# Per-row norm factor moved from the inputs to the exits of two projections, and the memory norm moved among the gate products

## The reference, cut to what matters

```python
# end of the first block
ple_gate = jax.nn.sigmoid(rms_norm(x, g_ple) @ w_ple_gate)
x = x + ple_gate * (p @ w_ple_proj)

# second block
mem_n = rms_norm_2(mem, mem_norm)
hn = rms_norm_2(h, norm_pre[0])                     # h = x
k_m, v_m = split(mem_n @ w_mem_kv[i])               # for both layers i
c_q, c_kv, k_r, q_m, gate = split(hn @ w_in_a)      # 384, 256, 32, 256, 1024 columns
main = mla_mixer(c_q, c_kv, k_r, ...)
mem_out = softmax(q_m @ k_m.T / 8) @ v_m            # 4 heads, 256 memory tokens
...
```

## Time and profile before

| | us |
|---|---|
| median of 3 runs (lowest, highest) | 3482.05 (3481.04, 3482.25) |
| the profiled execution | 3481.96 |
| its span | 3480.2 |
| TensorE busy | 3105.8 (89%) |
| VectorE busy | 1777.9 (51%) |
| ScalarE busy | 1185.4 (34%) |
| GpSimd busy | 1085.8 (31%) |
| mean granted TensorE clock | 0.953 |

### The profile page before, as it was taken

One profiled execution on the slowest core, in us unless ns is written; L12 is line 12 of the kernel. 1 busy time (PEld: TensorE's weight loads), 2 busy tenths in 40 slices (PEclk: granted clock), 3 DMA queues, 4 the chain that ended last, 5 costly groups with the idle time before them and its releaser, 6 DMA issues.

```text
span 3480.2 us, 36734 instructions
## 1 busy us (share of the span) xinstructions
PE 3105.8 (89%) x14488; PEld 2561.2 (74%) x14488; DVE 1777.9 (51%) x1804; ACT 1185.4 (34%) x1880; POOL 1085.8 (31%) x426
## 2 busy tenths in 40 slices
PE   5888799999999999999886898899976689999997
PEld 4666578887878888888676677688855567777786
DVE  5888943112253444444675334577744746656533
ACT  2666720001131000000322223577742425555511
POOL 2111034444424444444245232111122022121152
PEclk9999999999999999999898998999997899999998
DMA  2000021112101111111112111200031110000131
GB/s 94 19 25 31 19 91 49 49 49 93 46 31 49 49 49 49 49 49 49 43 49 106 34 67 52 79 31 25 31 127 43 49 37 26 30 25 31 55 115 67
DMA packets 44572, 178.99 MB, mean 51 GB/s; under 512 B 4672, under 2 KB 5696, under 8 KB 43392
## 3 DMA queue, kind: packets, MB, share of 16 engines
q1 hardware_dynamic: 32976, 119.89, 10.9%
q10 hardware_dynamic: 11440, 56.89, 4.2%
HBM read 147.40 MB, written 29.36 MB: 51 GB/s over the span
## 4 chain that ended last, share of the span: by engine, by line
PE 72%; DVE 11%; issue 10%; ACT 5%; POOL 2%; DMA 1%; SPq 0%; ACTq 0%; DVEq 0%; POOLq 0%
PE ps L456 47%; PE ps L1022 4%; PE aux L933 3%; PE ps L872 2%; PE ps L917 2%; PE ps L576 2%; PE ps L478 1%; PE ob L500 1%; PE ob L952 1%; PE ob L955 1%; PE ob L953 1%; PE aux L935 1%; DVE eb L1811 1%; POOL wh L413 1%; PE aux L605 1%
## 5 line engine op out<-in xcount | busy, mean ns | idle before, releaser
L413 POOL TENSOR_TENSOR wh<-raw,con 128x1024 fp32r<-128x1024 f32 x211 | 510.3, 2419 | 2334.1 <-PE ps L456 1198.9
L415 POOL TENSOR_TENSOR wl<-raw,wh 128x1024 fp32r<-128x1024 f32 x211 | 575.3, 2727 | 16.6
L456 PE MATMUL ps<-hh,wh 128*128 128x512 f32 x1536 | 479.7, 394 | 29.0 <-POOL wl L415 11.3
L456 PE MATMUL ps<-hl,wh 128*128 128x512 f32 x1536 | 477.4, 392 | 0.0
L456 PE MATMUL ps<-hh,wl 128*128 128x512 f32 x1536 | 476.4, 391 | 0.0
L456 PEld LDWEIGHTS ps<-hh,wh 128*128 128x128 f32 x1536 | 289.9, 190 | 92.1 <-issue 18.4
L456 PEld LDWEIGHTS ps<-hl,wh 128*128 128x128 f32 x1536 | 291.3, 190 | 61.4
L456 PEld LDWEIGHTS ps<-hh,wl 128*128 128x128 f32 x1536 | 291.0, 189 | 61.3
L1669 DVE TENSOR_TENSOR px_l<-px,px_h 128x512 fp32r<-128x512 f32 (+3 forms) x288 | 214.0, 745 | 115.4 <-ACT px_h L1526 113.3
L1909 DVE TENSOR_TENSOR y_t<-y_t,ps 128x1024 f32<-128x1024 f32 x120 | 146.5, 1220 | 174.6 <-PE ps L456 174.6
L1259 ACT ACTIVATE ff<-fr 128x1024 f32<-128x1024 f32 x32 | 34.0, 1061 | 552.9 <-DVE fr L1898 552.9
(11 more groups left out here) (353 smaller groups left out, 6291.3 us busy)
## 6 DMA issues: line engine op xcount, KB each, us to landing
raw<-wall SPq DMA_DIRECT2D x211, 512.0 KB, 3.5
spill_x<-x_t ACTq DMA_DIRECT2D x2, 4096.0 KB, 12.7
spill_out<-ot ACTq DMA_DIRECT2D x16, 512.0 KB, 2.6
go<-spill_out ACTq DMA_DIRECT2D x16, 512.0 KB, 5.8
xold_t<-spill_x ACTq DMA_DIRECT2D x2, 4096.0 KB, 16.4
x_t<-xt SPq DMA_DIRECT2D x8, 512.0 KB, 8.5
spill_o<-op ACTq DMA_DIRECT2D x4, 1024.0 KB, 3.9
o_all<-spill_o ACTq DMA_DIRECT2D x2, 2048.0 KB, 12.6
```

Source lines behind the costliest of these rows:

```text
L413: pool.tensor_tensor(wh[:, s, :, :], raw[:, s, :, :], ones.unsqueeze(1).broadcast_to([P, KT, P]), ALU.mult).then_inc(w_high, 1)
L415: pool.tensor_tensor(wl[:, s, :, :], raw[:, s, :, :], wh[:, s, :, :].bitcast(F32), ALU.subtract).then_inc(w_split, 1)
L456: m = pe.matmul(ps[:, w, a:b], lw[:, sl, k, :], r[:, i, a:b], start=(i == 0 and j == 0), stop=(i == len(ks) - 1 and j == 2))
```

## The change

- The gate products and the second block's first projection read x*g instead of x*g*r: `hh` is made on ACT straight from x and g (`Identity` with a scale), `hl` on DVE (`ple_low`, `scalar_tensor_tensor` of x, g and `hh`). The row is copied once to SBUF (`ple_row`, `a_row`) and multiplied in where a product leaves PSUM, now on DVE (`ple_scaled`, `q_scaled`, `scaled_out`, `gate_scaled`).
- The tiles `hh`, `hl` are made within `update`, so the gate products start tile by tile; the sums of the last two squares go between the k tiles (`with_late_sums`), the row between the last tile's two halves.
- The projection of `p` is taken out earlier, to `pp` (eight buffers of their own).
- The memory norm is done after the fourth gate product's exit (m = 3 on DVE and ACT, before the sixth k tile of gate product 4 on TensorE), with its own small buffers `mnt`.
- `hh`, `hl` for the second block are made while gate product 7 still reads the old ones (semaphore `gate_tile`, per k tile). Its two query products come before the memory products, and one by one.
- The memory values are computed with `m_h` as the stationary operand and the weights moving, 48 matmuls of 128 columns (`memory_values`), and need no transpose. The pads of the queries are cleared within that stretch.
- `cq`, `ckv`, the rope key and the gates of layer 0 leave by DVE.

```diff
@@ TensorE
-        norm_stats(KT, S, slab_next=True)
-        nready = norm_tiles(KT)
-        two_products(hh, hl, nready)
-        for _ in range(KT - 2):
-            product(range(KT), hh, hl)
-        pe.wait_ge(macc_ready, 1)
-        clear_sums(0)
-        column_sums(m_acc, N_MEM, 0).then_inc(mstat_done, 1)
-        tile_sums(KT, S, 1)
...
+        two_products(hh, hl, with_late_sums(norm_tiles(KT)), between=lambda: norm_row(S))
+        for m in range(2, KT):
+            product(range(KT), hh, hl, ready=(lambda i: norm_row(N_MEM) if i == 5 else None) if m == 4 else None,
+                    read=gate_tile if m == KT - 1 else None)
+            if m == 2:
+                pe.wait_ge(macc_ready, 1)
+                clear_sums(1)
+                column_sums(m_acc, N_MEM, 1).then_inc(mstat_done, 1)
+
+        mready, ready = norm_tiles(KT), norm_tiles(KT)
+        product(range(KT), hh, hl, ready=with_late_sums(ready))
+        product(range(KT), hh, hl, ready=lambda i: norm_row(S) if i == 1 else None)
         for layer in range(2):
             for j in range(2):
-                product(range(KT), m_h, m_l, n=N_MEM, ready=ready)
...
+                product(range(KT), m_h, m_l, n=N_MEM, ready=mready)
+                mready = None
             for j in range(2):
-                w = product(range(KT), m_h, m_l, n=N_MEM)
-                evacuated(w)
-                transposes(mv, 2, slab_next=(layer == j == 1))
+                memory_values()
@@ VectorE
+        def ple_low(k, gain=V_PLE):
+            dve.wait_ge(nh_ready, t.next(nh_ready))
+            dve.scalar_tensor_tensor(out=hl[:, k, :], in0=x_t[:, k, :], scalar=vcol(gain + k),
+                                     in1=hh[:, k, :].bitcast(F32), op0=ALU.mult, op1=ALU.subtract).then_inc(norm_ready, 1)
...
+        for i in range(2):
+            zero_pads(pads[i])
+            q_scaled(i)
+        for i in range(8):
+            memory_out(i)
...
+        def scaled_out(dst):
+            w, slot = work()
+            dve.tensor_tensor(dst, ps[:, slot, :], a_row[:, :], ALU.mult).then_inc(work_free[slot], 1)
...
-        skip()
+        gate_scaled(5, gt_late)
         w, slot = work()
+        chain(dve.tensor_tensor(ps[HI, slot, :], ps[HI, slot, :], a_row[HI, :], ALU.mult))
         norm(cq_t, 3, S, V_QN, cq_h, cq_l)
```

More of the change, by code:

```diff
@@ L460, in proj, with product, memory_values, two_products @@
                             t.fresh = False
+                if read is not None and k != ks[-1]:
+                    m.then_inc(read, 1)
             m.then_inc(work_done, 1)
-        def product(ks, rh, rl, n=S, ready=None, sl=None):
+        def product(ks, rh, rl, n=S, ready=None, sl=None, read=None):
             sl = slab() if sl is None else sl
             w, slot = work()
-            proj(slot, sl, ks, rh, rl, n, ready)
+            proj(slot, sl, ks, rh, rl, n, ready, read)
             return w
-        def two_products(rh, rl, ready, begun=True):
+        def memory_values():
+            sl = slab()
+            w, slot = work()
+            for kb in range(2):
+                rows = slice(kb * P, (kb + 1) * P)
+                for k in range(KT):
+                    for j, (l, r) in enumerate(((m_h, wh), (m_l, wh), (m_h, wl))):
+                        m = pe.matmul(ps[:, slot, rows], l[:, k, rows], r[:, sl, k, :],
+                                      start=(k == 0 and j == 0), stop=(k == KT - 1 and j == 2))
+                        if t.fresh:
+                            m.then_inc(slab_begun, 1)
+                            t.fresh = False
+            m.then_inc(work_done, 1)
+        def two_products(rh, rl, ready, begun=True, between=None):
             slabs, slots = [slab(), slab()], [work()[1], work()[1]]
@@ L483, in two_products @@
                         m.then_inc(work_done, 1)
+                        if between and i == 0:
+                            between()
         def transposes(src, n, slab_next=False):
@@ L1679, in norm_row, with square_adder @@
             dve.wait_ge(row_done, t.next(row_done))
-        def square_adder(ktiles):
+        def square_adder(ktiles, late=1):
             first = t.take("sq", ktiles)
+            total = acc if ktiles == KT else cq_acc
             def add(k):
@@ new lines, in _, with ple_scaled, ple_added @@
+        update(y_t, x_t, x_t, V_POSTMLP, low_part=ple_low, squares=square_adder(KT, 2))
+        ple_low(KT - 1)
+        skip(KT)
+        norm_row(S)
+        chain(dve.tensor_copy(ple_row[:, :], row[:, :]))
+        def ple_scaled(m):
+            w, slot = work()
+            if m >= 2:
+                dve.wait_ge(tile_ready, tiles + m - 1)
+            dve.tensor_tensor(pg[m % 2][:, :], ps[:, slot, :], ple_row[:, :], ALU.mult).then_inc(work_free[slot], 1)
+        def ple_added(m):
+            dve.wait_ge(ple_ready, m + 1)
+            chain(dve.tensor_tensor(pg[m % 2][:, :], pg[m % 2][:, :], pp[m], ALU.mult))
+            dve.tensor_tensor(x_t[:, m, :], x_t[:, m, :], pg[m % 2][:, :], ALU.add).then_inc(tile_ready, 1)
@@ L1932, in _ @@
             if m > 1:
                 squares(m - 1)
-        barrier(dve, t, dve_end)
-        norm(m_t, KT, N_MEM, V_MEM, m_h, m_l)
+            if m == 3:
+                norm_row(N_MEM, 1)
+                norm_tiles(m_t, KT, N_MEM, V_MEM, m_h, m_l, tmp=mnt)
+                t.take(norm_ready, KT)
+            if m == KT - 2:
+                for k in range(KT - 2):
+                    ple_low(k, V_PRE2)
+        ple_low(KT - 1, V_PRE2)
+        norm_row(S)
+        chain(dve.tensor_copy(a_row[:, :], row[:, :]))
@@ new lines, in q_scaled @@
+        def q_scaled(n):
+            w, slot = work()
+            for h, rows in ((0, LO), (1, HI)):
+                i = dve.scalar_tensor_tensor(out=q_f[n][rows, h, :], in0=ps[rows, slot, :], scalar=SCALE_64,
+                                             in1=a_row[rows, :], op0=ALU.mult, op1=ALU.mult)
+            i.then_inc(work_free[slot], 1)
+            dve.wait_ge(high_ready, t.next(high_ready))
+            for h, rows in ((0, LO), (1, HI)):
+                low(pads[n][1][rows, h, :], q_f[n][rows, h, :], pads[n][0][rows, h, :])
```

208 lines of the change are left out of this document (127 added, 81 removed).

## The result

| | before | after |
|---|---|---|
| median (lowest, highest), 15 runs each, us | 3482.12 (3478.40, 3488.31) | 3490.63 (3485.83, 3498.34) |
| the profiled execution, its span, us | 3481.96, 3480.2 | 3489.53, 3487.6 |
| mean granted TensorE clock | 0.953 | 0.948 |

The ratio is 1.0025, 95% interval 1.0018 to 1.0032: 8.5 us slower, just above what I called no change and 0.6 us above my range. I had forecast 4 us faster.

A forecast was written before the change was run, and what follows sets the result against it. TensorE, busy 89% of the span, was taken as the bound, so only its waits and low clock could be won. Terms -14.4 up to the scores, +1.3 and +9.0 gave -4.1: 3478.0 us, range 3465 to 3490.

The forecast's parts named there:

- the price of a value matmul: Memory values: 0.11 to 0.13 us for each of 48 matmuls, so 6.1 us a product (first 7.0).
- The marks of my sum: Predicted start times on TensorE, moved one after another; the memory scores at 1932.4 against 1946.86.
- The rival that I wrote down with this mechanism: Value products run at the low clock, 0.22 us a matmul, 17 us more: 3495; chance 0.15.
- the last mark: Start of the first latent product, after the memory attention; predicted shift -4.1 us.
- Up to the third gate product: Stretch ending where the third gate product starts: 9.5 us earlier, at 1764.8 against 1774.31.
- The memory norm: Norm within gate product 4: 5.9 us lost, with 3.8 of wait and 1.0 for a lower clock.
- The chain of the exits: Queries: DVE's row copy, pad clears, scaling and remainders free slot 1 at P+60, when the second key product starts.
- The attention: Memory attention: 1.3 us lost; five gate spills each 0.27 later behind DVE's exits, 1.35.
- My 1.5 back for a warm start: Memory attention: starting with TensorE warm returns the 1.5 us of loading the exponential's table at the first maximum.
- After it: After the memory attention: 9.0 us lost, from gate 5's exit behind the angles, rope key scaling and later gate exits.
- the clock rival: Value products at the low clock, 0.22 us a matmul, 17 us more: 3495; chance 0.15.
- The prediction's title for the stretch after the gate products: Heading for the stretch from the gate products' end to the memory attention: 10.5 us won.

The follow-up runs named there:

- e5_before_direct: Kernel before with only its memory value products replaced by 48 matmuls of 128 columns, no copy or transposes: 3496.55 us, ratio 1.0043.
- e6_before_wide: Kernel before with only its memory value products replaced by direct ones of 256 moving columns: 3486.06 us, ratio 1.0009.
- e1_turned: Kernel after with memory values again computed as 24 matmuls of 256 columns, copied out by ScalarE and transposed: 3471.84 us, ratio 0.9971.
- e2_wide: Kernel after with the 48 value matmuls taking 256 moving columns in place of 128, for all but the last input block: 3475.34 us, ratio 0.9980.

## Why the prediction was wrong

- **The failed step** is the price of a value matmul: "I take 0.11 to 0.13, as each matmul has its own load and keys, half idle, ran mostly at the high clock." Measured: 0.21 for nearly all of them. My own upper bound, "the low clock on a weight-bound stream, 3.55/16 = 0.22", from column sums in that very stretch, was the right row. I chose the row of the attention, where such matmuls are few and stand among wide ones, and leaned on keys that are 256 columns wide. The marks of my sum held 25.4 us for the four, the first at 7.0; the two pairs took 19.7 and 19.9. With these in their place the scores come 0.2 us earlier than before; the trace has 0.9 later. The rival that I wrote down with this mechanism, its price (17 us) and its result (3495) had 0.15. It deserved far more: rows of the stretch spoke for both clock levels, and none of them was a sustained stream of 128 columns. Of the 14.8 us between forecast and trace at the last mark, the value products are 14.2; the smaller misses below nearly cancel.
- The Trainium skill (TensorE: Matmul & The Clock Gate, Back-to-back issue gap) has some 81 ns for a pair of weight load and matmul at 128 columns. The trace does not agree: 0.11 us at the high clock, 0.21 at the low. By the page I would have been wrong by 5 us more.
- **Up to the third gate product**: -8.5 for -9.5, right. **The memory norm**: the wait is 3.43 us for my 3.8, but the gate products as a whole took 7.0 us more for my 5.9. I had read the earlier trace rows as a multiply that ended with the split `wh`; by the rows it ended at 1801.80 and the split at 1800.72, 1.1 us earlier. ScalarE's rows again have the root 0.01 us behind the end of the table load, so the drain of 1.38 us that the Trainium skill names (ScalarE: Activation LUTs, What ACT_TABLE_LOAD costs) is not seen here either:

```profile
1796.69 1.28 ACT L1145 ACT_TABLE_LOAD   x1 [5.11 <-DVE acc L1759]
1797.98 0.26 ACT L1145 ACTIVATE small<-ob,con 128x2 f32<-128x2 f32 x1
```

- **The chain of the exits**: the gate products end at 1837.1, and with P the start of the last of them (10.9 us earlier) the second key product starts at P+59.5 for my P+60, the first value product at P+67.5 for my 68.3. The keys of the second layer took 10.9 us for my 10.8. Everything around the failed term in this stretch was right to a microsecond. The match of the keys is in part luck: the first of them ran at the low clock, which I had not priced there, and took 5.55 us, as long as the pace of the splits that I had counted (5.4).
- **The attention** lost 2.7 us for my 1.3, and the reason that I gave is not what the runs show: e5_before_direct and e6_before_wide keep the exits of the kernel before and take 2.4 and 2.2 us more than it from the scores to the last values. My 1.5 back for a warm start is not seen either: in e1_turned and e2_wide the first scores run at 0.12 us, and the same way takes 170.3 and 169.7 us, more than the 168.0 of the kernel after. Why is open.
- **After it** 7.0 were lost for my 9.0. The queue behind gate 5 is worth 4.4 of them, for which I had 4.4 and 1.2 at the low clock; the exit of gate 6 ahead of the second norm accounts for nearly all of the rest.
- **The range** ended at 3490 because I left out "the worst third of the clock rival". A bound that a row of the same stretch supports should have stayed in. (The prediction's title for the stretch after the gate products, 10.5 us won, does not match its own marks, which give 10.7; nothing hangs on that.)

## What to carry to other kernels

When a change swaps wide matmuls for narrower ones with as many or more weight loads, ask what TensorE's clock will do before counting matmuls: here 128 columns per weight load cost 0.21 us each for as long as the stream lasted, and 256 columns 0.12 once the clock had come back, so doing twice the columns was faster. Where rows give a price at both clock levels and no row shows the new stream, carry both prices through the sum and let the range hold both. And when an exit moves to another engine, follow the queue of the engine that it left: the spill that stayed on ScalarE still waited for the exit, and held up the squares behind it.

## What the runs showed of the hardware that I had not expected

- A stream of 128-column matmuls, each with its own weights and TensorE busy 19.3 of 20 us, ran at a granted 0.54 and did not recover in 96 matmuls; the same stream at 256 columns recovered within the product, and its second pair ran at 1.00. Being busy did not bring the clock back by itself.
- In another place the same narrow stream kept 0.11 us for a whole product. Why is open.
- At the low clock a matmul with its own weights cost 0.21 us at 128 and at 256 columns alike, at the high one 0.11 and 0.12.
- Two remainders of a query pair on VectorE took 6.13 us where POOL split beside them and 2.45 where it did not.
